# The prompt's attention values on column halves of TensorE, with row sums on GpSimd and a new pacing of the streams' attention

## The reference

```python
# forgetting attention, 8 heads of 64; c is the running sum of log forget values
logits = einsum('bqhd,bkhd->bhqk', qi, k) * scale
logits = logits + cq[..., :, None] - ck[..., None, :]
p = softmax(where(mask, logits, -inf))
o = einsum('bhqk,bkhd->bqhd', p, v)
...
# delta rule, 4 heads of 128: state S is carried from chunk to chunk
delta = ui - einsum('bhck,bhkv->bhcv', wi, S)
o = einsum(qi * exp(Gi), S) + einsum(ai, delta)
S = S * exp(g_last) + einsum(ki * exp(g_last - Gi), delta)
```

## Time and profile before

| | us |
|---|---|
| median of 3 runs | 3775.36 |
| their extremes | 3775.32 and 3775.93 |
| the profiled execution's own time | 3776.01 |
| its span in the trace | 3774.3 |
| TensorE busy | 3626.1 |
| VectorE busy | 1607.2 |
| ScalarE busy | 1171.0 |
| GpSimd busy | 337.3 |

### The profile page before, as it was taken

One profiled execution on the slowest core, in us unless ns is written; L12 is line 12 of the kernel. 1 busy time (PEld: TensorE's weight loads), 2 busy tenths in 40 slices (PEclk: granted clock), 3 DMA queues, 4 the chain that ended last, 5 costly groups with the idle time before them and its releaser, 6 DMA issues. The chain is left out here.

```text
span 3774.3 us, 54542 instructions
## 1 busy us (share of the span) xinstructions
PE 3626.1 (96%) x20888; PEld 3159.2 (84%) x20888; DVE 1607.2 (43%) x3505; ACT 1171.0 (31%) x2318; POOL 337.3 (9%) x416
## 2 busy tenths in 40 slices
PE   8999999899999999998879999999999999999998
PEld 8999999777776677776668889999999999888886
DVE  4000277755544544444534444444444444432222
ACT  5122122333333333332323333333333333321111
POOL 3000000211211121121200000000000000000000
PEclk9999999899999999999979999999999999999999
DMA  4212322312221022015543321111111111432222
GB/s 157 71 62 64 83 70 70 81 36 48 47 61 41 25 59 51 17 57 179 174 145 120 126 72 46 44 46 46 46 46 46 46 46 35 153 126 82 81 82 69
DMA packets 328131, 278.90 MB, mean 74 GB/s; under 512 B 97218, under 2 KB 292914, under 8 KB 326893
## 3 DMA queue, kind: packets, MB, share of 16 engines
q1 hardware_dynamic: 318319, 258.03, 23.0%
q0 software_dynamic: 5216, 18.23, 1.4%
q10 hardware_dynamic: 4416, 0.14, 0.1%
HBM read 190.70 MB, written 85.65 MB: 73 GB/s over the span
## 5 line engine op out<-in xcount | busy, mean ns | idle before, releaser
L2643 PE MATMUL bank<-ffn_hn_hi,ffn_w_parts 128*128 128x436 f32 (+1 forms) x3520 | 987.5, 361 | 2.4 <-ACTq L2750 2.4
L2643 PEld LDWEIGHTS bank<-ffn_hn_hi,ffn_w_parts 128*128 128x128 f32 x3520 | 662.2, 188 | 39.3 <-issue 2.8
L2643 PE MATMUL bank<-ffn_hn_lo,ffn_w_parts 128*128 128x436 f32 (+1 forms) x1760 | 634.7, 361 | 0.0
L416 PE MATMUL bank<-in_xh,in_wh 128*128 128x436 f32 (+1 forms) x1280 | 357.6, 360 | 3.1 <-DVE in_wh L634 3.1
L2643 PEld LDWEIGHTS bank<-ffn_hn_lo,ffn_w_parts 128*128 128x128 f32 x1760 | 331.3, 188 | 19.4
L2677 PE MATMUL bank<-ffn_down_wa,ffn_g_hi 128*128 (+1 forms) x1224 | 328.8, 391 | 3.3 <-DVE ffn_g_lo L2972 3.3
L2779 ACT COPY ffn_raw<-bank 128x436 f32<-128x436 f32 (+1 forms) x220 | 110.5, 502 | 705.4 <-PE bank L2643 650.8
L1571 PE MATMUL bank<-heads_p_pT,heads_p_v 128*65 128x512 f32 (+3 forms) x640 | 287.0, 530 | 10.3 <-issue 9.9
L2906 DVE TENSOR_SCALAR ffn_hist<-ffn_raw 128x2 f32 (+2 forms) x264 | 44.9, 170 | 549.1 <-ACT ffn_acc L2783 546.4
L2677 PEld LDWEIGHTS bank<-ffn_down_wa,ffn_g_hi 128*128 128x128 f32 x1224 | 230.0, 188 | 52.8 <-DVE ffn_down_wa L2969 3.3
L416 PEld LDWEIGHTS bank<-in_xh,in_wh 128*128 128x128 f32 x1280 | 241.3, 189 | 14.9 <-DVE in_wh L634 3.5
(11 more groups left out here) (424 smaller groups left out, 6199.3 us busy)
## 6 DMA issues: line engine op xcount, KB each, us to landing
ffn_w<-in_w_up_dram SPq DMA_DIRECT2D x44, 512.0 KB, 5.0
ffn_g_raw<-scratch_g SPq DMA_DIRECT2D x110, 192.0 KB, 2.3
scratch_g<-ffn_acc SPq DMA_DIRECT2D x88, 218.0 KB, 2.0
heads_s_k<-in_cache_fox_k_dram SPq DMA_DIRECT2D x8, 2048.0 KB, 13.9
heads_s_v<-in_cache_fox_v_dram SPq DMA_DIRECT2D x8, 2048.0 KB, 8.3
heads_d_qkvT<-scratch_gch SPq DMA_DIRECT2D x17, 768.0 KB, 5.8
ffn_y<-in_w_down_dram SPq DMA_DIRECT2D x22, 512.0 KB, 3.4
scratch_gch<-in_work SPq DMA_DIRECT2D x48, 218.0 KB, 1.9
```

Source lines behind the costliest of these rows:

```text
L416: mm = pe.matmul(bank[:, 4 + i % 2, 0:wide], a[:, k, :], b[:, k, col:col + wide], start=(k == 0 and m == 0), stop=(k == KD - 1 and m == 2))
L2643: mm = pe.matmul(bank[:, pair(n) + e, 0:width], w_parts[a][:, part, e, k, :], x[:, k, cols], start=(k == 0 and m == 0), stop=(k == KD - 1 ...
```

## The change

- The values' multiplication takes four key blocks at once. Even blocks give their 64 rows on partitions 0 to 63 of the result's bank, odd ones on 64 to 127. The column of ones is gone.
- `pT` has eight buffers in the place of three; they lie in the memory of `S_s`, which is free in that time. SP waits for the end of the prompt's attention before it loads the states there.
- GpSimd adds up the exponentials of a group's blocks in `acc` (128x512), a new generator `sums_gpsimd`. The delta rule's program on GpSimd gets due times and is woven with it.
- Per group a new use "z" of the two banks: four transpositions of `acc`, which VectorE reduces to sums and inverts. The output is turned with 128 rows in the place of 65, and VectorE adds the two halves before it multiplies.
- `set_times` prices a column at `1.81e-3`, with 2.0 in the place of 1.6 a group, and keeps uses of the same bank 1.8 units apart.
- The streams begin 13 units after the prompt's end, and all their due times within a stream are stretched by `PACE = 1.4`.

```diff
@@ Delta.sync
             if t == NC - 2:
+                sp.wait_ge(self.prompt.s["row_free"], len(self.prompt.uses))
                 sp.dma_start(self.S_s[:].rearrange("p b h n -> p (b h) n"),
@@ Delta.gpsimd: a yield ahead of each step
         for t in range(self.NC + 1):
+            late = self.start(t) + self.ROOTS
+            yield self.start(t) + 5.0
             pool.wait_ge(s["sumsq_ready"], t + 1)
             inverse_root(self.unit, self.ss, EPS, 2 * GH, "unit_ready", t)
+            yield late + 9.0
             pool.wait_ge(s["scaled_ready"], 5 * t + 2)
...
+            yield late + 14.3
             pool.wait_ge(s["lt_ready"], 2 * t + 1)
...
+                yield late + 17.4
                 output(t - 1)
+            yield late + 22.0
             weigh_z(t)
+        yield self.last_at(self.NC) + 28.0
         output(self.NC)
@@ Prompt
+    NPT, AT_ONCE = 8, 4
...
-        self.v = ph.sb("p_v", [P, 2, NB, FD + 1])
+        self.v = ph.sb("p_v", [P, 2, NB, FD])
...
-        self.pT = ph.sb("p_pT", [P, 3, BANK])
-        self.oT, self.inv, self.o = ph.sb("p_oT", [FD + 1, BANK]), ph.sb("p_inv", [P, 2, 4]), ph.sb("p_o", [P, 2, 4, FD])
+        self.pT = lent[:].rearrange("p b h n -> p (b h n)").rearrange("p (u n) -> p u n", n=BANK)
+        self.acc = ph.sb("p_acc", [P, 2, BANK])
+        self.oT, self.inv, self.o = ph.sb("p_oT", [P, BANK]), ph.sb("p_inv", [P, 2, 4]), ph.sb("p_o", [P, 2, 4, FD])
@@ Prompt.set_times
-            return 2.65e-3 * sum(self.width(G, b) for b in range(self.blocks(G))) + 0.95e-3 * first + 1.6 + \
+            return 1.81e-3 * sum(self.width(G, b) for b in range(self.blocks(G))) + 0.95e-3 * first + 2.0 + \
                 (0.5 * 4 if G % self.NG in (1, 2) else 0.0)
...
+        self.summed = [self.first_key[G] - G + max(b, 1) for G, b in self.key_at]
...
-            uses.append((self.key_at[G, self.blocks(G) - 1] + 7.6, ("o", G)))
+            uses.append((self.key_at[G, self.blocks(G) - 1] + 8.0, ("z", G)))
+            uses.append((self.key_at[G, self.blocks(G) - 1] + 9.0, ("o", G)))
...
-        self.uses = sorted(uses)
+        self.uses = []
+        for at, tag in sorted(uses):
+            self.uses.append((max(at, self.uses[-2][0] + 1.8) if len(self.uses) >= 2 else at, tag))
@@ Prompt.rows_tensor
+        def turn_row_sums(r, G):
+            pe.wait_ge(s["p_summed"], self.summed[self.first_key[G] + self.blocks(G) - 1])
+            for i in range(4):
+                mm = pe.transpose(self.row_bank(r)[:, i * P:(i + 1) * P], self.acc[:, G % 2, i * P:(i + 1) * P], ident)
             mm.then_inc(s["row_mm"], 1)
@@ Prompt.values_tensor
-            u, wide, last = self.first_key[G] + b, self.width(G, b), self.blocks(G) - 1
+            first, last, FD = b - self.AT_ONCE + 1, self.blocks(G) - 1, self.FD
+            if b % self.AT_ONCE != self.AT_ONCE - 1:
+                continue
             yield at + 4.0
-            if b == 0:
+            if first == 0:
                 pe.wait_ge(s[f"v_loaded{h % 2}"], 16 * (h // 2) + 16)
                 after(pe, s["oT_ready"], G)
-            pe.wait_ge(s["p_ready"], u + 1)
-            pe.matmul(self.bank[0:self.FD + 1, self.out, BANK - wide:BANK], self.v[:, h % 2, b, :],
-                      self.pT[:, u % 3, BANK - wide:BANK], start=(b == 0), stop=(b == last)).then_inc(s["pv_mm"], 1)
+            pe.wait_ge(s["p_ready"], self.first_key[G] + b + 1)
+            for n in range(first, b + 1):
+                half, cols = n % 2, slice(BANK - self.width(G, n), BANK)
+                mm = pe.matmul(self.bank[half * FD:(half + 1) * FD, self.out, cols], self.v[:, h % 2, n, :],
+                               self.pT[:, (self.first_key[G] + n) % self.NPT, cols], start=n < 2, stop=n >= last - 1)
+            mm.then_inc(s["pv_mm"], 1)
@@ Prompt.keys_scalar
-            after(act, s["pv_mm"], u - 2)
+            if u >= self.NPT:
+                act.wait_ge(s["pv_mm"], (u - self.NPT) // self.AT_ONCE + 1)
+                act.wait_ge(s["p_summed"], self.summed[u - self.NPT])
@@ Prompt, new
+    def sums_gpsimd(self, pool):
+        s, nc = self.s, self.nc
+        for (G, b), at in self.key_at.items():
+            u, wide, acc = self.first_key[G] + b, self.width(G, b), self.acc[:, G % 2, :]
+            cols, p = slice(BANK - wide, BANK), self.pT[:, u % self.NPT, :]
+            if b == 0:
+                continue
+            yield at + 5.0
+            pool.wait_ge(s["p_ready"], u + 1)
+            if b == 1:
+                if G >= 2:
+                    pool.wait_ge(s["row_mm"], self.use["z", G - 2] + 1)
+                before = self.pT[:, (u - 1) % self.NPT, :]
+                if wide < BANK:
+                    nc.gpsimd.tensor_copy(acc[:, 0:BANK - wide], before[:, 0:BANK - wide])
+                nc.gpsimd.tensor_tensor(acc[:, cols], before[:, cols], p[:, cols], ALU.add).then_inc(s["p_summed"], 1)
+            else:
+                pool.wait_ge(s["p_summed"], self.summed[u] - 1)
+                nc.gpsimd.tensor_tensor(acc[:, cols], acc[:, cols], p[:, cols], ALU.add).then_inc(s["p_summed"], 1)
@@ Prompt.vector
+        def row_sums(r, G):
+            inv = self.inv[:, G % 2, :]
+            dve.wait_ge(s["row_mm"], r + 1)
+            nc.vector.tensor_reduce(inv, self.row_bank(r).rearrange("p (n k) -> p n k", k=P), AX.X, ALU.add) \
+                .then_inc(s["row_free"], 1)
+            dve.wait_ge(s["row_free"], r + 1)
+            nc.vector.reciprocal(inv, inv).then_inc(s["inv_step"], 1)
...
+            nc.vector.tensor_reduce(self.o[:, a, first:], turned[:, first:].rearrange("p n e d -> p n d e"), AX.X, ALU.add) \
+                .then_inc(s["inv_step"], 1)
+            dve.wait_ge(s["inv_step"], 2 * G + 2)
+            tt(self.o[:, a, first:], self.o[:, a, first:], spread(inv[:, first:].unsqueeze(2), [P, 4 - first, FD]), ALU.mult) \
                 .then_inc(s["row_free"], 1)
@@ Sample
-    PERIOD = 33.0
+    PACE = 1.4
+    PERIOD = 33.0 * PACE
...
-        self.prompt, self.begin = prompt, prompt.end + 9.0
+        self.prompt, self.begin = prompt, prompt.end + 13.0
...
-                yield at + 25.0 + 0.7 * n
+                yield at + self.PACE * (25.0 + 0.7 * n)
@@ project_and_heads
-            d.gpsimd(pool, (lambda: p.edges(pool, 1), lambda: p.edges(pool, 2)))
+            weave(d.gpsimd(pool, (lambda: p.edges(pool, 1), lambda: p.edges(pool, 2))), p.sums_gpsimd(pool))
```

More of the change, by code:

```diff
@@ L1499, in logits @@
             if G in (0, self.NG) and i == 0:
-                pe.wait_ge(s["edges_ready"], 7 if G else 4)
+                pe.wait_ge(s["edges_ready"], 6 if G else 3)
             if g == 0 and i == 0:
@@ L2079, in vector @@
             for n, due in enumerate((6.6, 12.6, 13.0)):
-                yield at + due
+                yield at + self.PACE * (due)
                 logits_out(b, n)
@@ L2142, in project_and_heads @@
         whole, ph.stack = ph.stack, first
-        p = Prompt(ph, nc, c, io, bank, (3, 4, 5, 6, 7), r, t, (tok, f, before), prj)
+        p = Prompt(ph, nc, c, io, bank, (3, 4, 5, 6, 7), r, t, (tok, f, before), d.S_s, prj)
         ph.stack = whole
+    d.prompt = p
     t.place(lambda n, *shape: ph.sb("s_" + n, *shape), p, d.S_s)
```

92 lines of the change are left out of this document (50 added, 42 removed).

## The result

The kernel takes 3795.99 us (median of 4 runs, 3790.99 to 3801.74) beside 3775.64 (3775.32 to 3776.97) for the kernel before: a ratio of 1.0056, interval 1.0043 to 1.0068. The forecast was 3751.5, with 3708 to 3804 as range. So the size lies in the range, but the sign is the other one: 20 us slower where 24 us faster was the likeliest. The profiled execution took 3793.62 with a span of 3791.9.

The account below looks back on a forecast made before the run. The prediction took TensorE, busy 96% of the span, as the bound. The prompt's stretch at 807 us plus a later one of 355 gave 1162 against 1186, 24 less: 3751.5 us, range 3708 to 3804.

Parts of the forecast that it names:

- The values on halves: Prompt's value matmuls on TensorE: 234 us become 123 side by side, plus 26 us for going into and out of halves.
- The rival of serial halves (E): Prompt's value halves run one after another on TensorE: 111 us more than forecast, 3863 us; chance 0.05.
- the rival in which the idle time falls (B): Prompt's stretch fills to 94%, a lone delta tile takes 54 us: 71 us less, 3704; chance 0.19.
- More for TensorE, and the waits: Prompt's stretch: 14 us for turning sums, 6 for wider output transpositions, 6 for new waits, 15 off for old ones.
- with a quarter of the waits I take 15 off: TensorE's 24.2 us idle before the prompt's values shrinks, saving 15 us (8 to 19).
- The shorter schedule: Prompt ends at 807 units instead of 975; 2.33 delta tiles, 56 us of work, move behind it; stretch 948 to 807 us.
- If the filling stays at 90%: Cross-check of the prompt's stretch: 731 us of TensorE work take 812 us; 778 at 94%, 840 at 87%.
- The later stretch: Behind the prompt: 4.65 delta tiles of 57 us and an end of 90, 355 us against 238.
- GpSimd: Its 288 sums in the prompt's stretch take 305 us (250 to 369), all hidden while the queue stays in step.
- C: GpSimd's in-order queue holds the delta rule, 5.1 us more per tile, 55 us over 10.74 tiles: 3806; chance 0.17.
- All given back: Later delta tiles keep 61 us and the end its 99, so no change: 3779 us; chance 0.15.

Follow-up runs that it names:

- e4_whole: Changed kernel with the values back on the whole array, still four blocks at once, output not the reference's: 3879.58 us (ratio 1.0282).
- f2_before_squeezed: Kernel before with only the changed kernel's plan (prompt ends at 807 units, bank spacing 1.8, streams' start and pacing): 3794.47 us (1.0056).
- f3_no_z: Changed kernel without row sums on GpSimd, their transpositions or their reduction, inverse set to one: 3750.96 us (0.9939).
- h4_streams_extra_after: Changed kernel with 32 unread 512-column matmuls added between the 16-column ones of the streams' delta tile: 3787.52 us (1.0032).
- h1_extra: Changed kernel with 60 unread 512-column matmuls added in the prompt's stretch: 3803.56 us (1.0068).
- after: The changed kernel itself, against the kernel before the change: 3795.99 us (1.0056).
- e3_no_sums: Changed kernel with GpSimd's sums replaced by one memset to 1 per group, transpositions kept: 3775.98 us (1.0003).
- the control: Kernel before under the changed kernel's plan, with VectorE's row maxima over a quarter of the columns: 3782.17 us (1.0019).
- before: The kernel without the change, the reference for all ratios: 3775.64 us.
- g3_ones: Changed kernel with sums turned by matmuls against one column of ones, without VectorE's 512-column reduction: 3807.85 us (1.0086).
- h3_streams_extra: Kernel before with 32 unread 512-column matmuls added between the 16-column ones of the streams' delta tile: 3773.53 us (0.9992).

## Why the prediction was wrong

**The values on halves** (234 to 123 and 26): right, 143 measured for 149. The saving of 85 us is what `e4_whole` shows in the time, 84. The rival of serial halves (E) is out, and so is the rival in which the idle time falls (B): the stretch holds 725 us of work (731 less these 6) in 850, a filling of 85%.

**More for TensorE, and the waits**, is the step that failed. The prediction gave everything that comes with the halves 14 us for turning the sums, 6 for wider output transpositions and 6 for all waits, and took off 15 because the values' own waits go ("with a quarter of the waits I take 15 off"): 11 us together. They cost 85, the distance from `f2_before_squeezed` to `e4_whole`; by the mean clocks (0.9838 and 0.9795) at most 18 of them can be the clock. Leaving out sums and turning gave 45 of them back (`f3_no_z`) where the prediction had 14 and 6. The transpositions themselves cost what was said or little more (the four of an output 0.49 us, 1026.69 to 1027.18). But the turning also takes a row bank, which VectorE must first free and then read for 0.68 us. The values' own waits did go (0.0 us before line 1598), and others took their place: the row logits' went from 5.5 to 18.8 us in nine tiles, the delta rule's matmuls took 17 us more. What makes up the other 40 of the 85 us was not told apart; the grouping by four is a suspect that no run tests alone.

**The shorter schedule**, by itself, was better than forecast, and here two errors offset each other. My terms for it make the stretch 881 us and the later one 355, which is 50 us slower than before with no saving at all; it cost 20 (`f2_before_squeezed`). The forecast of -24 is thus -85 for the halves, 11 for the companions and 50 for the plan; the runs show -84, 85 and 20. The time fell within the range by luck: had the plan cost its 50, it would have been some 3826. "If the filling stays at 90%" took the filling for a property of the stretch. Squeezed, the kernel before reached 796 us of work in 860, 93%; with less work and the companions it fell to 85%, below the 87% that I took as the end. The squeezed plan is not why: under the old one halves with sums bring nothing either, 3774.07 beside 3773.94.

**The clock** had no term at all. Both profiles showed it (0.93 in the later window). It went from 0.9867 to 0.9805 on the mean, worth 24 us at most. `h4_streams_extra_after` shows that it costs time in the streams' delta tile: there the same matmuls run in 236 ns instead of 354, and the kernel is faster with more work. In the prompt's stretch it is a correlation: `h1_extra` did not lift it.

**The later stretch**: 355 forecast, 356 measured (358 to the very last values). 353 of it come with the plan alone.

**GpSimd** (C): the sums took 1.29 us where 1.27 was taken, and without them the kernel is 20 us faster. C's 3806 is the nearest of the rivals' times, 10 us off, and its sign came true, tiles 78.8 us apart where it named 78 or more. Its mechanism did not: `f2_before_squeezed` has no sums and tiles 79.9 us apart (808.4 to 1607.0), so the delta rule's chain is not what they hold: from the first X to the last step of XT a tile takes 36.4 us in after, 37.0 in `f2_before_squeezed` and 36.1 in `e3_no_sums` (worked out from the ends of lines 1112 and 1261, mean of tiles 2 to 10), and 11 of the 20 us are the difference of the clock column (74 to 63). How GpSimd's sums reach the clock stays open. VectorE's instruction with two SBUF inputs (line 1643) took 690 ns in the middle and 1827 at the longest, while a sum ran (line 1689, 1038.87 to 1040.16); the longest in `f2_before_squeezed` is 1395. It runs 32 times and explains a few us.

**All given back** (D) had the sense of it, the saving lost, but at 3779 and behind the prompt's stretch; it was lost within it. That the companions cost as much as the halves save was in no rival.

What stays open: the price of the pieces doesn't add up to a sum. Leaving out the sums is worth 20, the turning 25, shorter maxima 20 (8 beyond the control), and twice as many mode changes cost 10; some of it is the same time counted twice, and how much was not told apart. With halves but without sums and turning the kernel reaches 3751, but it leaves out work that the outputs need.

## What to carry to other kernels

A schedule written in due times and a cheaper operation are two changes: run the old kernel under the new schedule as well, or a loss of the one hides in the other. Add a run that has everything that comes with the cheaper operation and not the operation itself: here that run (`e4_whole`) showed that the operation saved what was forecast and its companions took it all. And price what a small added step holds besides its engine, a bank or another engine's pass, since work that fills a wait is not saved when it gets shorter. Look at the granted clock too before you compare kernels a few tenths of a per cent apart: time multiplied by clock gives the other end of what the difference can be.

## What the runs showed of the hardware

- Two column halves fed with two-pass float32 matmuls run side by side: eight passes of 512 columns in 1.87 us with the way out, 3.44 one after another (`after`, `before`). The way in added 0.09 us (`after` against `e4_whole`).
- Four float32 matmuls of one column, eight passes, took 0.81 us at least until the next instruction started (`g3_ones`), four transpositions of 128 columns 0.35 (`after`).
- A stretch with 118 passes of 16 columns on whole-array weights ran at half of TensorE's clock for 34 us with TensorE busy for 32.5, 354 to 365 ns each; in one profiled execution with a 512-column matmul behind every second matmul they took 236 ns at a clock of 1.00 (`h4_streams_extra_after`), and the kernel was 8.5 us faster with the more work. In another kernel with the same addition (`h3_streams_extra`) the clock fell all the same for 30.7 us.
- With the granted clock of ten runs of one kernel between 0.986 and 0.993, its time went from 3785.7 to 3761.5.
